# A hybrid decoder step on one core: sample queries computed as rows, the first sample's turn moved ahead of the loop, prompt heads one turn later

## What is computed

```python
mod = silu(c) @ w_ada + b_ada                       # six modulation vectors
h = rms_norm(x, g_norm1) * (1.0 + sc1) + sh1
q, k, v, glu_a, glu_b, gate_a, gate_c = split(h @ w_in)   # 512,512,512,512,512,1024,1024 columns
q, k = rms_norm(q, g_q), rms_norm(k, g_k)           # per head, 8 heads of 64
attn = moba_attention(q, [k_cache, k], [v_cache, v]) @ w_attn_proj
u = glu_a * sigmoid(glu_b)
cv = silu(layer_norm(depthwise_conv(u, 31 taps))) @ w_conv_proj
x = x + gt1 * ((sigmoid(gate_a) * attn + sigmoid(gate_c) * cv) @ w_out)
x = x + gt2 * swiglu_ffn(rms_norm(x, g_norm2) * (1.0 + sc2) + sh2)   # inner width 2816
```

## Time and profile before

| what | before |
|---|---|
| runs, median (lowest, highest) | 586.12 us (584.86, 587.48) |
| span of the profiled execution, first to last instruction | 584.0 us |
| busy: PE, DVE, ACT, POOL | 523.6, 394.2, 292.1, 170.0 us |
| mean granted clock of TensorE over the span | 0.958 of 2.4 GHz |
| moved by DMA | 159.31 MB, mean 273 GB/s |

### The profile page before, as it was taken

The page is one execution under the profiler, slowest core; times in us unless marked ns, Lnnn a source line. Parts: engine busy times, 40 slices in busy tenths (PEclk is TensorE's granted clock), DMA queues, the critical chain, the costliest instruction groups (busy, mean ns, idle before and its releaser), DMA issues.

```text
span 584.0 us, 10410 instructions
## 1 busy us (share of the span) xinstructions
PE 523.6 (90%) x4180; PEld 441.1 (76%) x4180; DVE 394.2 (67%) x602; ACT 292.1 (50%) x519; POOL 170.0 (29%) x232
## 2 busy tenths in 40 slices
PE   3769899988979879798798999899999999999997
PEld 3658678865655646556458888799999999999996
DVE  1742674789999998999765865567565656554441
ACT  3144433587777877655653532293444444434331
POOL 8326377287778776750100000000000000000000
PEclk9589898897999999999979999999999999999999
DMA  8999459698999999999676989946466446476501
GB/s 306 370 369 388 165 189 346 224 357 296 405 399 397 420 401 416 366 366 414 260 296 245 387 291 374 364 148 213 150 221 206 147 158 164 122 192 169 153 20 38
DMA packets 82128, 159.31 MB, mean 273 GB/s; under 512 B 2573, under 2 KB 61113, under 8 KB 76952
## 3 DMA queue, kind: packets, MB, share of 16 engines
q1 hardware_dynamic: 76256, 89.27, 45.8%
q0 software_dynamic: 5120, 67.71, 28.9%
q10 hardware_dynamic: 703, 1.67, 0.8%
HBM read 156.39 MB, written 2.72 MB: 272 GB/s over the span
## 4 chain that ended last, share of the span: by engine, by line
PE 57%; DVE 21%; DMA 10%; issue 5%; ACT 4%; POOL 1%; SPq 1%; ACTq 1%; DVEq 0%; POOLq 0%
PE acc L1580 12%; PE acc L1581 12%; PE acc L1582 12%; DVE prod L1057 7%; DMA wring<-in_w_in 6%; DVE sall L1064 4%; PE acc L1452 3%; DMA wring<-in_w_ffn_in 2%; PE acc L1465 2%; PE acc L1467 2%; PE acc L1466 2%; DMA pr<-in_page_table 2%; PE acc L1384 2%; PE chain L1604 2%; ACT L623 1%
## 5 line engine op out<-in xcount | busy, mean ns | idle before, releaser
L1129 DVE TENSOR_TENSOR wlo<-wring,whi 128x1024 fp32r<-128x1024 f32 (+2 forms) x84 | 92.0, 1097 | 72.2 <-ACT whi L623 71.4
L623 ACT ACTIVATE whi<-wring 128x1024 fp32r<-128x1024 f32 (+2 forms) x84 | 80.1, 958 | 83.2 <-PE acc L1582 77.4
L1580 PE MATMUL acc<-xlo,whi 128*128 128x264 f32 x384 | 110.2, 287 | 3.5 <-DVE wlo L1129 1.3
L1581 PE MATMUL acc<-xhi,wlo 128*128 128x264 f32 x384 | 108.8, 283 | 0.0
L1582 PE MATMUL acc<-xhi,whi 128*128 128x264 f32 x384 | 108.8, 283 | 0.0
L578 POOL TENSOR_TENSOR cvT<-cvT,cprod 128x256 f32<-128x256 f32 x120 | 87.9, 732 | 42.4 <-ACT cprod L623 27.6
L1452 PE MATMUL acc<-hT,wring 128*128 128x264 f32 x336 | 92.1, 418 | 3.7 <-DMA wring<-in_w_in 3.3
L1580 PEld LDWEIGHTS acc<-xlo,whi 128*128 128x128 f32 x384 | 72.3, 188 | 5.8 <-issue 3.1
L1452 PEld LDWEIGHTS acc<-hT,wring 128*128 128x128 f32 x336 | 63.3, 200 | 17.6 <-DMA wring<-in_w_in 3.7
L1064 DVE TENSOR_REDUCE sall<-prod 128x32 f32<-128x2048 f32 x32 | 73.0, 2281 | 0.4
L1581 PEld LDWEIGHTS acc<-xhi,wlo 128*128 128x128 f32 x384 | 72.4, 188 | 0.1
(11 more groups left out here) (316 smaller groups left out, 913.4 us busy)
## 6 DMA issues: line engine op xcount, KB each, us to landing
wring<-in_w_ffn_in SPq DMA_DIRECT2D x22, 1024.0 KB, 7.7
wring<-in_w_ada SPq DMA_DIRECT2D x20, 1024.0 KB, 15.3
wring<-in_w_in SPq DMA_DIRECT2D x12, 1024.0 KB, 11.3
wring<-in_w_ffn_out SPq DMA_DIRECT2D x16, 704.0 KB, 5.6
more<-in_w_out SPq DMA_DIRECT2D x4, 1024.0 KB, 13.7
more<-in_w_ada SPq DMA_DIRECT2D x4, 1024.0 KB, 12.5
wring<-in_w_in SPq DMA_DIRECT2D x6, 512.0 KB
wring<-in_w_in SPq DMA_DIRECT2D x4, 768.0 KB
```

Of the source, the lines that this page charges most:

```text
L623: return nc.scalar.activation(out, in_, f, **kw)
L1129: v.tensor_tensor(wlo[:, place, 0:n, :], w, whi[:, place, 0:n, :].bitcast(F32), ALU.subtract)\
L1580: mm(bank[:, 0:R], whi[:, place, k - k0, :], lo[:, k, :], start=k == 0, stop=False)
L1581: mm(bank[:, 0:R], wlo[:, place, k - k0, :], hi[:, k, :], start=False, stop=False)
```

## The change

Five things are changed, all of them in the order of work up to the end of the loop.

1. **Queries as rows.** When the q weights have landed, PE multiplies the samples' eight activation rows with the whole 512 columns of q weights (`rows_of_queries`, 8 f32 matmuls of 512 columns in four column groups of the array), ACT copies the four parts, one matmul adds them up (`sum_of_rows`, in the middle of tile q0), and DVE and ACT normalise the rows. The transposes, the small matmuls and the copies of before are gone. POOL's key gather 0 moves ahead of its first `rest`.
2. **Sample 0's turn** (block choice, mask, maximum, exponentials, sum) is moved in between the tiles v0 to b0 ahead of the loop, with sample 1's scores; the norms of the k heads come ahead of those of the q heads. The loop now has turns 1 to 7. `weigh_values(0)` stands in turn 1.
3. **Prompt heads a turn later.** Turn b does head b-1. Turn 7 does head 6, and head 7 behind it.
4. **Wide gate loads.** The sixteen gate tiles come in four slots of four tiles, the other a and b tiles in one slot `glu1`. Three tiles are computed in each turn 1 to 7 (`EARLY`, `FIRST`, `SECOND`), g15 at the very end (`LAST`). a1 and b1 are no longer split.
5. **Key places.** Chunks 0 to 3 use the two places in `kring` alone, and from chunk 4 on all three are used in turn. The convolution's taps are in turns 1 to 6.

```diff
-THIRD = {0: "a2", 1: "b2", 2: "a3", 3: "b3", 4: "g10", 5: "g13"}
-FIRST_GATE = (0, 2, 4, 6, 8, 11, 14)
...
+EARLY = {1: "a1", 2: "b2", 3: "g0", 4: "g3", 5: "g6", 6: "g9", 7: "g12"}
+FIRST = {1: "b1", 2: "a3", 3: "g1", 4: "g4", 5: "g7", 6: "g10", 7: "g13"}
+SECOND = {1: "a2", 2: "b3", 3: "g2", 4: "g5", 5: "g8", 6: "g11", 7: "g14"}
+LAST = "g15"
+STREAM = {"a1": ("glu", 1), "b1": ("glu", 3), "a2": ("glu1", 0), "a3": ("glu1", 1), "b2": ("glu1", 2), "b3": ("glu1", 3)}
...
+def key_place(chunk):
+
+    return chunk % 2 if chunk < 4 else (chunk + 1) % K_PLACES
...
-                        pool.wait_ge(k_used, STEPS // CH * (chunk - K_RING + 1))
-                    gather(k_place[chunk % K_RING], cache_k, k_full[chunk % K_RING], chunk // CH, chunk % CH)
+                    if KEY_BEFORE[chunk] is not None:
+                        pool.wait_ge(k_used, STEPS // CH * (KEY_BEFORE[chunk] + 1))
+                    if chunk == 4:
+                        pool.wait_ge(acc_full, NUMBER[LAST_FILL["k"]] + 1)
...
             pool.wait_ge(acc_full, NUMBER["vec"] + 1)
-            pool.wait_ge(w_full[0], 64)
+            pool.wait_ge(w_full[1], 64)
+            gather_k(0)
+            pool.wait_ge(rows_full, 1)
 
...
-            for name in ON_POOL:
+            for _, _, name in SPLITS:
                 rest(name)
-                if name == "q1":
-                    gather_k(0)
-                if name == "k0":
+                if name == "q2":
                     gather_k(1)
-                if name == "v0":
-                    pool.wait_ge(acc_full, NUMBER[LAST_FILL["k"]] + 1)
+                if name == "k3":
                     gather_k(2)
+                if name == "v1":
+                    gather_k(3)
+                    gather_v(0, 0)
                 if name == "v2":
-                    gather_k(3)
-                if name == "v3":
-                    gather_v(0, 0)
-                if name == "b1":
                     gather_k(4)
-            for b in range(B):
+            gather_k(5)
+            gather_k(6)
+            pool.wait_ge(acc_full, NUMBER["b0"] + 1)
+            gather_v(0, 1)
+            for b in range(1, B):
                 add_taps(b, 0)
-                if b == 0:
-                    pool.wait_ge(acc_full, NUMBER["b1"] + 1)
-                    gather_v(0, 1)
-                else:
+                if b >= 2:
                     for c in range(CH):
                         gather_v(b, c)
                 add_taps(b, 1)
+                if b == 1:
+                    for c in range(CH):
+                        gather_v(b, c)
...
+                    exponentials(B - 1)
                     conv_rows()
-                act.wait_ge(pp_ready, b + 1)
-                func(oT[DH * j:DH * j + DH, i, 0:S], psO[DH * j:DH * j + DH, 0:S], ACT.Copy).then_inc(po_ready, 1)
-                if b < B - 1:
-                    gate(FIRST_GATE[b] + 1)
+                prompt_out(hd)
+                column(SECOND[b])
                 if b == B - 2:
                     root("lnv", C, lnf)
-
-            values(B - 1)
+            scale_rows(B - 1)
+            turned_rows(B - 1)
+            column(LAST)
+            prompt_out(B - 1)
+            values_out(B - 1)
+            split_weights(AHEAD)
+            split_weights(AHEAD + 1)
+            values_turned(B - 1)
 
...
+                    step_pr = head_scores(B - 1)
+                    dve.wait_ge(dve_step, step_pr)
+                    mark(v.tensor_reduce(pmx[:, 0:1], pr[:, 0:P], AX.X, ALU.max, negate=True))
+                    v.tensor_reduce(pmx[:, 1:2], pr[:, P:384], AX.X, ALU.max, negate=True).then_inc(pb_ready, 1)
...
+            def rows_of_queries(w):
+
+                pe.wait_ge(h_rows, 1)
+                for k in range(KD):
+                    q = k % 4
+                    ins = mm(psS[32 * q:32 * q + 32, :], hs[:, k, :], w[:, k, :], start=k < 4, stop=k >= 4)
+                ins.then_inc(rows_full, 1)
+
+            def sum_of_rows():
+
+                pe.wait_ge(consts, 3)
+                pe.wait_ge(rows_copied, 1)
+                mm(psT[0:32 + B, :], pick[:, :], rowparts, start=True, stop=True).then_inc(rows_summed, 1)
+
             w = slot_ready("q")
-            tile("q0", w, 0, hT)
+            rows_of_queries(w)
+            tile("q0", w, 0, hT, k1=2)
+            sum_of_rows()
+            tile("q0", w, 0, hT, k0=2)
             split("q1")
+            pe.wait_ge(qs_ready, 1)
+            pe.wait_ge(qlo_ready, 1)
+            spread_query(0)
             split("q2")
             head_sums(0)
             split("q3")
             head_sums(1)
-            split("k0", k1=2)
-            pe.wait_ge(qsq_ready, 1)
-            mm(chain[:, 0:32], halves[:, :], qsq.rearrange("p t b -> p (t b)"), start=True, stop=True).then_inc(qsq_summed, 1)
-            split("k0", k0=2, k1=6)
-            pe.wait_ge(qsn_ready, 1)
-            for t in range(4):
-                nc.tensor.transpose(psS[0:B, P * t:P * t + P], qsn[:, t, :], ident[:, :])
-                ins = mm(psS[32:32 + B, P * t:P * t + P], qsn[:, t, :], ident[:, :], start=True, stop=True)
-            ins.then_inc(qs_turned, 1)
-            split("k0", k0=6)
-            split("k1", k1=3)
-            pe.wait_ge(qs_ready, 2)
-            pe.wait_ge(qlo_ready, 1)
-            spread_query(0)
-            split("k1", k0=3)
...
-                if b < B - 1:
-                    tile(f"g{first}", mix, 0, hT, k0=4)
...
+                column(EARLY[b], k0=4 if b >= 2 else 0, k1=7)
+                sample_mask(b)
+                if b == B - 1:
+                    prompt_scores(B - 1)
+                column(EARLY[b], k0=7)
+                sample_maxima(b)
+                column(FIRST[b], k1=4)
+                if b == 1:
+                    weigh_values(0)
+                sample_max_spread(b)
+                column(FIRST[b], k0=4)
+                if b == 1:
+                    turn_values(0)
...
+                turn_rows(hd)
...
+                column(SECOND[b], k1=5)
+                sample_total(b)
+                prompt_values(hd)
+                column(SECOND[b], k0=5)
...
-                if b in THIRD:
-                    tile(THIRD[b], mix, 2, hT, k1=4)
+                    prompt_scores(b)
+                    column(EARLY[b + 1], k1=4)
+            turn_rows(B - 1)
+            column(LAST)
+            prompt_values(B - 1)
```

More of the change, by code:

```diff
@@ L251, in program @@
         samples = pg[:, :, :].rearrange("p g h -> p (g h)")
-        qsn, qsq, qroot = (samples[:, 32 * e:32 * e + 32].rearrange("p (t b) -> p t b", t=4) for e in range(3))
         wsel = samples[:, 96:96 + 30]
@@ L382, in conv_part @@
         def conv_part(b, part):
-            if b >= CONV_LOOPS:
+            if b not in CONV_PARTS:
                 return range(0)
-            first = CONV_PART * b + sum(CONV_SPLIT[:part])
-            return range(first, first + CONV_SPLIT[part])
+            return range(CONV_FIRST[b, part], CONV_FIRST[b, part] + CONV_PARTS[b][part])
         @block.sync
@@ L426, in load @@
                 elif kind == "glu":
[L427 to L433 removed]
+                    parts = [(full[:, :, 2 * P * e:2 * P * e + 2 * P], cols(w_in, glu0 + C * e + 2 * P * num, 2 * P)) for e in range(2)]
+                elif kind == "gt":
+                    parts = [(full, cols(w_in, glu0 + 2 * C + 4 * P * num, 4 * P))]
                 elif kind in ("conv", "attn"):
@@ L726, in _ @@
-            square("k", 3)
-            high("v1")
+            square("q", 3)
+            high("k3")
+            for t in range(4):
+                raw("k", t)
+                square("k", t)
+                high(f"v{t}")
             raw("v", 0)
             act.wait_ge(sq_used, 8)
-            func(headsums, small[0:2 * H, 0:R], ACT.Sqrt, scale=1.0 / DH, bias=eps[0:2 * H, :]).then_inc(head_root, 1)
-            high("v2")
+            func(headsums, chain[0:2 * H, 0:R], ACT.Sqrt, scale=1.0 / DH, bias=eps[0:2 * H, :]).then_inc(head_root, 1)
@@ L752, in glu, with column @@
                     freed(func(cvT[:, t, :], bank[:, 0:R], ACT.Sigmoid), f"b{t}")
+            def column(name):
+                if name[0] == "g":
+                    gate(int(name[1:]))
+                else:
+                    glu(name[0], int(name[1:]))
+            rows_out("ks", krow)
+            wait_freed(act, "ks")
+            act.dma_start(k_sample.rearrange("b o h d -> b (o h d)"), krow).then_inc(kept, 16)
             glu("a", 0)
+            bank = when_full(act, "so")
+            freed(func(sown[:, :, :].rearrange("p b h -> p (b h)"), bank[:, 0:B * H], ACT.Copy), "so")
+            act.wait_ge(s2_ready, 1)
+            func(s1[:, :, :], s1[:, :, :], ACT.Exp).then_inc(e_ready, 1)
             glu("b", 0)
@@ L1625, in _ @@
                     weigh_values(b - 1)
[L1627 to L1634 removed]
+                sample_gate(b)
@@ L1648, in _ @@
-                for e in range(QU):
```

(8 more changed lines are left out.)

545 lines of the change are left out of this document (295 added, 250 removed).

## The result

The changed kernel takes 597.07 us (median of five runs, 596.08 to 608.67), the kernel before 587.09 us beside it: a ratio of 1.021, with an interval of 1.017 to 1.026. In a second measurement the ratio was 1.012 (1.006 to 1.018). These ratios leave out a kernel's slow runs, which were six of the changed kernel's ten in the second measurement; the medians of all runs there, 600.92 and 586.29 us, stand at 1.025. The change makes the kernel slower. Both kernels vary from run to run (in the second measurement 589 to 603 us for the changed one, and 584 to 592 us for the one before, with a single run of 603.62), and the profiled execution took 602.74 us, 5.7 us more than the median, with a span of 601.0 us.

The account below looks back on a forecast made before the run. VectorE was taken to pace six loop turns, TensorE the stages before and after. From a span of 584.0 us, 16.0 of lead left came off and 20.7 for turn 7 were added: 588.7, so 590.8 us measured, range 579 to 602.

Parts of the forecast that it names:

- the case: Whole kernel: the lead won ahead of the loop is more than eaten by turn 7, slower; chance 0.36.
- The front: Ahead of the loop: first score at 53 us, sample 2's first multiply at 108.5 instead of 131.7, a lead of 23.2 us.
- (a) Turn 1: Turn 1: `weigh_values(0)` between the maximum and its spreading, and an exponential, add 2.7 us, of 0 to 4.
- (b) Turn 2: Turn 2: sample 1's values land late, TensorE waits 4.5 us; adds 2.5 us, of 0 to 5.
- (c) Turn 6: Turn 6: the taps now run into it and VectorE waits for them; adds 2.0 us, of 0 to 4.
- Turn 7: Last loop turn, with tiles and head 7 added: 39.5 us, 20.7 more than 18.8; bounds 35 and 45.
- The last stage: From `conv_unit(0)` to the end: stays 282.5 us as before.
- the base of turns 1 to 6: Loop turns 1 to 6: VectorE's work is what it was, so 151.0 us before the three additions.
- the wide loads themselves cost and save nothing: Gate loads: the bytes are the same, and the turn between a slot's release and its use hides them.
- transfers become the bound: Loop: turns 2 to 5 each wait 2.5 us for values, 600.8 us, slower; chance 0.12.
- TensorE's clock: Turn 7, the skill's rule: idle gaps throw TensorE back to half speed and the next work runs cold.
- the rival of 5.8 us: End of turn 7: g15, head 7's values and last weighing at half clock, 16.9 instead of 11.1 us; 596.6 us, chance 0.05.
- Table loads: Turn 7, the skill's rule: a drain beside each of three loads, 4.1 us more, 594.9 us; chance 0.02, slower.

Follow-up runs that it names:

- e1: The changed kernel without an edit, measured again against the kernel before: ratio 1.012.
- e2: The changed kernel with six products of the taps on ScalarE ahead of the copy `pvm<-chain` in turns 2 to 6, instead of seven or eight: 603.63 us, ratio 1.026.
- e5: The changed kernel with the gather of key chunk 7 asked for ahead of the second part of turn 1's taps instead of behind it: 591.15 us, ratio 1.006.
- e6: The changed kernel with `weigh_values(0)` behind the whole of tile b1 instead of in its middle, so gt0 is issued earlier: 592.06 us, ratio 1.006.
- e8: The changed kernel with the edits of e5, e6 and e7 together: 590.96 us, ratio 1.006.
- e10: The changed kernel with the edits of e5 and e9: 582.35 us, ratio 0.995.
- e11: e10 with the taps spread otherwise: 20 in turn 1, 23 in turns 2 to 5, 8 in turn 6: 582.60 us, ratio 0.992.
- e9: The changed kernel with ScalarE's order in turn 7 changed: head 6's output and head 7's rows ahead of the convolution's rows: 590.57 us, ratio 1.006.
- e7: The changed kernel with tile g15 ahead of head 7's transposes on TensorE at the end of turn 7: 601.07 us, ratio 1.023.
- e3: The kernel before, with seven and five products of the taps in a turn's first two parts instead of six and six: 590.86 us, ratio 1.008.

## Why the prediction was right, and where it was off

The forecast was slower, at 590.8 us in a range of 579 to 602; measured were 597.1. The sign and the case were right: the lead of the front is real, and is more than eaten. Term by term:

- **The front.** First multiply 53, measured 53.59. Sample 2's first multiply 108.5, measured 109.70; the lead is 22.0 us instead of 23.2.
- **(a) Turn 1.** 27.8 us against 25.6 in the kernel before, so 2.2 of the 2.7 us forecast.
- **(b) Turn 2.** TensorE was to wait 4.5 us for sample 1's values; it waited 3.67, at 143.55 us. GpSimd asked for them at 126.9, forecast was 125.
- **(c) Turn 6.** VectorE waits 1.3 us for the last tap; forecast was 2.0.
- **Turn 7.** Forecast 39.5 us, measured 37.6. The forecast chain is the one in the trace: TensorE waits 7.39 us (forecast 7 to 8) behind ScalarE's convolution rows, and g15 takes 6.29 us at a mixed clock (forecast 5.3).
- **The last stage.** 282.5 forecast, 282.9 measured.
- **The term that was wrong** is the base of turns 1 to 6: "VectorE's work in them is what it was, so 151.0 us", and with it "the wide loads themselves cost and save nothing". With the additions that made 158.2 us; measured were 170.8 in the first profile and 169.6 in e1, so 12 us more. VectorE's work is indeed what it was (147.2 us against 146.5), but it no longer sets the pace alone. I had named the condition, that a turn lies between a slot's release and its use, and I had worked out the date at which "the two chunks and the gate slot" would have landed as if they shared the queue in the order of issue. They don't. In e2 the gathers had 88% of the engines and the weights 13% while both had work, so that 2.1 MB of weights took 47 us and not 16. With one gather out of the way, in e5, turns 1 to 6 last 158.5 us, and the forecast was 158.2. That match is luck in part, since e5's profiled run took 2.4 us less than its median: in e6, e8, e10 and e11, which have no wait for gt0 either, they last 162.1 to 164.1 us. So of the 12 us the late load is about 5.5 to 11, and the rest goes mostly with the turns at half clock. The forecast had reckoned with a low clock in turn 7 alone; in turns 1 to 6 the granted clock is 0.86 in the first profile, where it was 0.97 before.

So 12 us were left out in turns 1 to 6 of the profiled execution, which was one of the long ones; the runs' median lies 6.3 us above the forecast. The rest of the sum is borne out by e5, which has the changed kernel's work without the late load: 591.15 us, a ratio of 1.006, against 590.8 us forecast, a ratio of 1.008. The rival "transfers become the bound" had the right resource and the wrong place: it expected waits of 2.5 us for values in each of four turns, and in five of the six profiles with this order of loads the largest loss is one wait for one load of weights.

The first profile shows no wait for gt0, and yet the load was as slow there. It was issued at 127.4 us, and the weights' queue had moved its 2.1 MB only at 166 us, 38 us later. TensorE came to tile g0 at 167.3 us, where it came at 158.7 us in e2 and 161.4 in e1: sample 1's values had come 3.67 us late, the rest of turn 2 ran at a low clock (0.74 in the turn), and the turn came to 32.5 us in all. That is 5 us more than the 27.7 us forecast for this turn. Another 7 us are lost in turns 3 to 5, which last 27.3 to 27.7 us at a granted clock of 0.81; the forecast had 25.2 each. So of the two causes of the 12 us it is the low clock that this profile shows, and the late load that most of the others show.

Two rules were weighed in the prediction. TensorE's clock: behind the wait of 7.39 us g15 took 6.29 us instead of the 3.73 of e9, but the last weighing was back at 3.62 us, so that only the transposes and a part of the tile ran cold. So the rival of 5.8 us came to 2.6. The Trainium skill (TensorE: Matmul & The Clock Gate, HAM oscillation) warns of work that runs cold behind a gap, and the trace agrees for the tile right behind it, with 6.29 us against 3.73. Table loads: in the changed kernel the sample's exponential starts 0.01 us after the load of 1.28 us ends.

```profile
294.21 0.39 ACT L640 ACTIVATE gates<-acc 128x264 f32<-128x264 f32 x1 [2.76 <-PE acc L1533]
294.62 1.28 ACT L640 ACT_TABLE_LOAD   x1
295.91 0.32 ACT L640 ACTIVATE s<-s 128x136 f32<-128x136 f32 x1
```

By the Trainium skill (ScalarE: Activation LUTs, What ACT_TABLE_LOAD costs) a switch of tables costs a drain of 1.38 us beside the load. The measurement decides: the load itself starts 0.02 us behind the gate's output, so that there is no drain on either side of it on this path.

## What to carry to other kernels

When work is moved, date each transfer by its own queue: what else is in flight from its issue to its use, and who wins. The load issued amid a burst of gathers took 40 to 47 us here, where all bytes in front of it and its own had asked for 16. An idle stretch of DMA in front of a burst was worth more than its length: with one gather moved into it the kernel took 10 us less than e7, which has the old order of loads on the same chip and one other edit. The packet counts of the two queues, beside their bytes, showed here why the gathers won. And where several chains end on one in-order engine, put the piece first that another engine stands waiting for: the same work in another order made the last turn 8 us shorter. Before giving up a change that moves work early and comes out slower, look where the lead is lost; here two moves of a few lines turned a ratio of 1.02 into 0.995. What was tried on top of them (0.992 twice) can't be told apart from that.

## What the runs showed of the hardware

The two DMA queues didn't share by bytes. With the weights' queue and the gathers' queue both full (e2, 133 to 160 us) they moved nearly the same number of packets, 679 and 683, of 2.0 KB and 14.7 KB on average, which is 13% and 88% of the engines' time. The two halves of a load of 2 MB took 25.9 and 46.7 us to land there, against 5.1 and 14.1 us in e6, where it was issued ahead of the gathers. That it is the packets that are shared out is read from these counts; no run changed a packet's size.

TensorE's clock did not fall alike after like waits: with 1.36 to 1.40 us idle ahead of `turn_values` the mask ran at half clock (1.05 us) in some turns and at full clock (0.60 us) in others, in e3 and e5 both kinds within one profile. With 0.9 us or less idle there it was at full clock, but for turn 2 of the first profile, in which TensorE had stood 3.67 us for values shortly before. What tells the two kinds apart was not found.
